# A two-layer decoder trunk on one core: stage changes rearranged, expert sums moved to TensorE, and unread matrix products placed in TensorE's gaps

## The chip, the cores and the metric

The kernel runs on one core of a Trainium2 chip. A core has five engines, each with its own instruction queue: TensorE (PE in the rows; its weight loads are PEld), VectorE (DVE), ScalarE (ACT), GpSimd (POOL) and SyncE (SP), which only starts transfers. They wait for one another by semaphores. The metric is the device time of one execution in microseconds, the median of three runs.

## The reference

The input is one sequence of 512 tokens of width 1024, in float32. There are two layers. Each is an attention part, a layer norm, a mixture of experts, and a second layer norm:

```
for i in range(DEPTH):
    mix = swa_sink_attention(...) if i % 2 == 0 else forgetting_attention(...)
    x = layer_norm(ALPHA * x + mix, ln_gain[i, 0], ln_bias[i, 0])
    ffn = grouped_moe(x, w_router, b_router, w_gate[i], w_up[i], w_down[i])
    x = layer_norm(ALPHA * x + ffn, ln_gain[i, 1], ln_bias[i, 1])
```

The router gives each token two of 16 experts and two gates. An expert computes `silu(x @ w_gate) * (x @ w_up)`, 256 wide, and multiplies that by `w_down`. The token's `ffn` is the sum of its two experts' rows, each times its gate.

## The kernel before

**Layout.** The 512 tokens are `NT = 4` tiles of 128 rows; `xres` holds them, 1024 columns each. Precise products of float32 data are made of three products of split operands (`three`, lines 491 to 493): high by high, high by low, low by high. `KC = 8` steps of three, 24 products of 512 columns, are one **group**. The splits are made by ScalarE (the high part, a cast) and VectorE (the low part, a subtraction).

**Order of a layer.** Input projection, attention, output projection (`wo_done`), first norm, routing, experts, second norm. After each tile's first norm TensorE transposes it (`turn_x`, line 477), and multiplies it by the router weights (`route`, line 648, products 16 columns wide). A long chain of small VectorE instructions then picks experts (`asn_b`, semaphore `assigned`), TensorE ranks the tokens by two products (674, 675), VectorE works out their places, TensorE turns these into row numbers (680), and GpSimd starts an indirect DMA for each expert (line 429) that fetches its 96 token rows from `xd` in HBM into `xe`. TensorE transposes the rows (`turn_rows`, 687), ScalarE and VectorE split them (`evac_rows`, lines 925 and 1336), and TensorE runs the gate and up products as one group of 24 (`gate_up_split`), the transposes of the hidden rows (706) and the down products (713, eight of 512 columns on plain float32).

**The expert loop.** A step `step(i, u)` has expert e's gate/up group, then the transposes for expert e+1 and the down products of expert e-1. The splits of expert e+1's weights are ScalarE's line 904 and VectorE's 1222, in four parts. The weights lie in a ring of four slots of 3 MB; SyncE's queue loads them ahead, in order, 1 MB each for gate, up and down. Between steps 2 and 3 ScalarE's queue has four instructions that multiply `xres` by ALPHA (line 959). Finished rows go to `ys` in HBM (line 920).

**After the experts.** GpSimd waits until all rows are stored, reads a counter (`n_ovf`), and gathers for each tile the two rows of each token (`gather`, line 458) into `gy`, with buffers for two tiles, so that the gathers of tiles 2 and 3 wait for `mixed`. VectorE adds the two, times their gates, to `xres` (lines 1415 and 1418), and norms (`norm`, 1027 to 1042); GpSimd computes the reciprocal root in two instructions (387, 388). In layer 0 the next layer's projection follows: `turn_x`, the split of the tile (`state_high`, `state_low`), and two groups of 24 products a tile. The projection's weights are split meanwhile (990 and `value_weights_low`, 1396). In layer 1 the four tiles are stored and the program ends. A branch for more than 96 tokens at one expert is in the program; the counter decides, and no row of the branch stands in the trace.

Of the kernel before, what the change touches and what calls it, by code (L numbers as in the profile page):

```python
# [48 lines left out]
def trunk(nc, x, ln_gain, ln_bias, swa_w_in, swa_sinks, swa_w_o, fox_w_in, fox_b_f, fox_w_o,  # L49
# [8 lines left out]
    with ctx:  # L58
# [95 lines left out]
        gy = area(0, 4 * D, "p (b k n) -> p b k n", b=2, k=2)  # L154
# [89 lines left out]

        block = ctx.enter_context(nc.Block())
# [3 lines left out]
        def _(eng):  # L249
# [33 lines left out]
            for l, (w_in, w_o) in enumerate(((swa_w_in[0], swa_w_o[0]), (fox_w_in[0], fox_w_o[0]))):  # L283
                for j in range(IN_BLOCKS[l]):
                    c = IN_ORDER[l][j]
                    if l == 1 and j == 2:

                        for b in range(2):
                            eng.wait_ge(S(f"gy_in0{b}"), 64)
# [53 lines left out]
        def _(eng):  # L343
# [39 lines left out]
            def norm_rstd(l, w, gather=None):  # L383
# [16 lines left out]
            for l in range(DEPTH):  # L400
# [30 lines left out]
                eng.wait_ge(S("placed"), l + 1)  # L431
                for b in range(2):
                    eng.wait_ge(S(f"y_stored{l}{b}"), 16 * NE // 2)
                n_ovf = eng.value_load(ovf_id[0:1, OVF:OVF + 1], min_val=0, max_val=OVF)
# [18 lines left out]
                def gather(t):  # L453

                    if t >= 2:
                        eng.wait_ge(S(f"mixed{l}"), t - 1)
                    for k in range(TOPK):
                        eng.indirect_dma_start(gy[:, t % 2, k, :], None, ys,
                                               bass.IndirectOffsetOnAxis(ap=pos[:, t, k:k + 1], axis=0)).then_inc(S(f"gy_in{l}{t % 2}"), 16)
                gather(0)  # L460
                gather(1)
                norm_rstd(l, 1, gather)


        @block.tensor
        def _(eng):
            def turn_x(t, a):
# [5 lines left out]
                if t >= 1:  # L473
                    eng.wait_ge(S(f"xt_act{a}"), t)
                    eng.wait_ge(S(f"xt_dve{a}"), t)
# [3 lines left out]
                mm.then_inc(S(f"xt_done{a}"), 1)  # L479

            eng.wait_ge(S("ident"), 1)
            turn_x(0, "in")
            for l in range(DEPTH):

                def xT_here(a, t):
                    eng.wait_ge(S(f"xt_act{a}"), t + 1)
                    eng.wait_ge(S(f"xt_dve{a}"), t + 1)

# [6 lines left out]
                if l == 0:  # L495
# [9 lines left out]
                    for j in range(IN_BLOCKS[0]):  # L505
                        for t in range(NT):
                            k = NT * j + t
                            xT_here("in", t)
                            if k >= 2:
                                eng.wait_ge(S(f"proj_free{l}{k % 2}"), k // 2)  # L510
                            for c in range(KC):
                                if k < NT - 1 and c == KC // 2:
# [9 lines left out]
                else:  # L522

                    turn_x(0, "01")
# [935 lines left out]
```

## Time and profile before

| | us |
|---|---|
| median of 3 runs | 988.99 (987.59 to 992.05) |
| the profiled execution | 988.5 |
| its span, first to last instruction | 986.6 |
| TensorE busy, of the span | 829.8 (84%) |
| VectorE / ScalarE / GpSimd busy | 547.7 / 383.9 / 136.1 |
| mean granted TensorE clock | 0.919 |

The granted clock is a share of 2.4 GHz; a stretch at 0.50 is one at 1.2 GHz. A window of the profile with, say, 0.54 has both levels in it. The mean of 0.919 says that TensorE had the lower level for about 16% of the span.

### The profile page before, as it was taken

Reading aid. Unit: us, or ns where it says so; the run is one execution under the profiler, and the core shown is the slowest. Engines: PE = TensorE matmul, PEld = TensorE weight load, DVE = VectorE, ACT = ScalarE, POOL = GpSimd, SP = SyncE. Lnnn points to the kernel's source line nnn. Section 1 sums busy time; section 2 is a strip of 40 time slices with the busy share of each in tenths; the row PEclk is TensorE's granted clock in tenths of the full one; section 3 lists DMA queues with packets and bytes.
Section 4 is the critical chain, followed back from the end, with each engine's and each line's share of the span. In section 5 each row is a group of like instructions: output and inputs, shape, how many; then the busy total and the mean of one; then the engine's idle time right before and its main releaser. Section 6 shows DMA issues by size and latency. Waiting matters only on the chain.

```text
span 986.6 us, 11641 instructions
## 1 busy us (share of the span) xinstructions
PE 829.8 (84%) x4140; PEld 601.7 (61%) x4140; DVE 547.7 (56%) x1086; ACT 383.9 (39%) x763; POOL 136.1 (14%) x153
## 2 busy tenths in 40 slices
PE   6999999981989999818999999999981889999910
PEld 4887777871546565417878877887861556556500
DVE  4534884556557676366332225664556556767437
ACT  4323884002455555231222226775001365555300
POOL 2000221121001000032000002221111100100033
PEclk9999999985899999959999999999985799999965
DMA  9942000149699998645062223111139599999144
GB/s 320 349 138 86 2 1 1 43 170 336 189 353 332 360 353 316 219 141 183 30 215 86 86 86 107 65 44 44 43 119 360 151 340 340 361 357 374 42 124 158
DMA packets 106851, 183.11 MB, mean 186 GB/s; under 512 B 6496, under 2 KB 72032, under 8 KB 106800
## 3 DMA queue, kind: packets, MB, share of 16 engines
q1 hardware_dynamic: 92864, 132.34, 39.7%
q0 software_dynamic: 9200, 33.33, 10.9%
q10 hardware_dynamic: 4736, 16.78, 4.5%
q8 instruction: 29, 0.48, 0.2%
q14 instruction: 22, 0.18, 0.1%
HBM read 159.60 MB, written 22.84 MB: 185 GB/s over the span
## 4 chain that ended last, share of the span: by engine, by line
PE 81%; DVE 9%; DMA 4%; issue 3%; POOL 2%; ACT 1%; POOLq 0%; DVEq 0%; SPq 0%; ACTq 0%
PE bank L491 16%; PE bank L492 16%; PE bank L493 16%; PE bank L713 12%; PE bank L613 5%; PE bank L579 4%; PE bank L596 3%; PE bank L687 2%; PE bank L477 2%; DMA arena<-xd,row_ids 1%; PE bank L648 1%; POOL veps L387 1%; DVE xres L1042 1%; DMA arena<-ys,pos 1%; PE bank L621 1%
## 5 line engine op out<-in xcount | busy, mean ns | idle before, releaser
L1222 DVE TENSOR_TENSOR low<-ring,gu_high 128x1024 fp32r<-128x1024 f32 x128 | 151.2, 1221 | 50.6 <-ACT gu_high L904 50.6
L904 ACT CAST gu_high<-ring 128x1024 fp32r<-128x1024 f32 x128 | 127.7, 1049 | 16.8 <-DVE arena L1353 16.8
L713 PE MATMUL bank<-ring,arena 128*96 128x512 f32 x256 | 119.8, 611 | 11.3 <-issue 9.2
L491 PE MATMUL bank<-gu_high,rows_high 128*96 128x512 f32 x256 | 115.4, 451 | 8.2 <-DVE rows_low L1336 8.2
L492 PE MATMUL bank<-low,rows_high 128*96 128x512 f32 x256 | 103.6, 405 | 0.0
L493 PE MATMUL bank<-gu_high,rows_low 128*96 128x512 f32 x256 | 103.0, 402 | 0.0
L713 PEld LDWEIGHTS bank<-ring,arena 128*96 128x96 f32 x256 | 40.1, 167 | 67.7 <-issue 67.3
L852 ACT ACTIVATE arena<-arena,nmax 128x256 f32<-128x256 f32 (+3 forms) x128 | 66.8, 522 | 30.8 <-DVE nmax L1153 20.0
L491 PE MATMUL bank<-high,x_high 128*128 128x512 f32 x160 | 66.2, 414 | 10.3 <-DVE low L1048 5.1
L414 POOL TENSOR_TENSOR low<-ring,high 128x512 fp32r<-128x512 f32 x32 | 40.6, 1269 | 231.1 <-ACT high L872 231.1
L613 PE MATMUL bank<-arena 128*128 128x64 f32 x544 | 68.1, 269 | 0.2 <-ACT arena L866 0.2
L613 PEld LDWEIGHTS bank<-arena 128*128 128x128 f32 x544 | 65.8, 192 | 0.5 <-ACT arena L866 0.5
L429 POOL DMA_INDIRECT arena<-xd,row_ids x32 | 30.2, 944 | 258.2 <-PE bank L687 220.0
L492 PE MATMUL bank<-low,x_high 128*128 128x512 f32 x160 | 64.7, 404 | 0.0
L493 PE MATMUL bank<-high,xlow 128*128 128x512 f32 x160 | 64.6, 404 | 0.0
L491 PEld LDWEIGHTS bank<-gu_high,rows_high 128*96 128x96 f32 x256 | 42.9, 167 | 33.3 <-DVE rows_low L1336 9.1
L492 PEld LDWEIGHTS bank<-low,rows_high 128*96 128x96 f32 x256 | 42.7, 167 | 23.7 <-issue 7.9
L493 PEld LDWEIGHTS bank<-gu_high,rows_low 128*96 128x96 f32 x256 | 42.7, 167 | 19.2 <-issue 0.9
L491 PE MATMUL bank<-high,attn_high 128*128 128x512 f32 x128 | 51.5, 402 | 0.0
L493 PE MATMUL bank<-high,attn_low 128*128 128x512 f32 x128 | 51.3, 401 | 0.0
L491 PE MATMUL bank<-x_high,wsplit 128*128 128x512 f32 x128 | 50.8, 397 | 0.0
L492 PE MATMUL bank<-xlow,wsplit 128*128 128x512 f32 x128 | 50.8, 397 | 0.0
(207 smaller groups left out, 1399.2 us busy)
## 6 DMA issues: line engine op xcount, KB each, us to landing
ring<-in_w_gate SPq DMA_DIRECT2D x32, 1024.0 KB, 12.3
ring<-in_w_up SPq DMA_DIRECT2D x32, 1024.0 KB, 14.4
ring<-in_w_down SPq DMA_DIRECT2D x32, 1024.0 KB, 12.7
ys<-arena ACTq DMA_DIRECT2D x32, 384.0 KB
ring<-in_fox_w_in SPq DMA_DIRECT2D x6, 2048.0 KB, 10.7
ring<-in_swa_w_in SPq DMA_DIRECT2D x3, 2048.0 KB, 8.8
ring<-in_swa_w_o SPq DMA_DIRECT2D x2, 2048.0 KB, 17.4
xd<-xres ACTq DMA_DIRECT2D x8, 512.0 KB, 2.6
```

Of the source, the lines that this page charges most:

```text
L414: eng.tensor_tensor(low, w, high, ALU.subtract).then_inc(S(f"out_low{l}"), 1)
L429: eng.indirect_dma_start(xe[0:CAP, e % RING, :], None, xd, bass.IndirectOffsetOnAxis(ap=row_ids[:, e:e + 1], axis=0)).then_inc(S(f"xe_in{l ...
L491: eng.matmul(out, ah, wh, start=(c == 0), stop=False)
L492: eng.matmul(out, ah, wl, start=False, stop=False)
L493: return eng.matmul(out, al, wh, start=False, stop=(c == KC - 1))
L579: mm = eng.matmul(s_bank(s, half)[:, 0:nk], QT[r, hp, n * P:(n + 1) * P], KT[r, kp, k0 * P:k1 * P], start=True, stop=(l == 0))
L596: mm = eng.transpose(bank[3 + half][:, i * P:(i + 1) * P], sp[:, 2 * (s % 2) + half, i * P:(i + 1) * P], ident[:, :])
L613: mm = eng.matmul(bank[5 + hp % 2][:, at:at + HD], pT[:, half, i * P:(i + 1) * P], (V0 if l == 0 else V)[:, k0 + i, v:v + HD], start=(i == ...
L713: mm = eng.matmul(bank[5 + half][0:CAP, :], hT[:, b, c, :], w[:, c, half * BLK:(half + 1) * BLK], start=(c == 0), stop=(c == FC - 1))
L852: eng.activation(p, p, ACT.Exp, bias=nmax[:, hp % 2, n, half:half + 1], scale=-1.0, accum_out=rsum[:, hp % 2, n, half:half + 1]).then_inc( ...
L904: eng.copy(gu_high[u % 2][:, part, :], slot_in(use)[:, part, :]).then_inc(S("gu_high"), 1)
L1222: eng.tensor_tensor(lows[use % RING][:, part, :], slot_in(use)[:, part, :], gu_high[u % 2][:, part, :], ALU.subtract).then_inc(S("gu_low"), 1)
```

## The change

All three stage changes (first norm to experts, experts to next layer, experts to output) are rewritten:

- **Sums on TensorE.** VectorE builds `gate_diag`, eight 128x128 diagonal matrices of the gates. TensorE multiplies them with the gathered rows (`mix_rows`, four plain float32 products of 512 columns a tile), and VectorE adds `ALPHA * xres` from PSUM in two halves, with the statistics of each half between. The multiplication by ALPHA on ScalarE (959) goes. `gy` has room for all four tiles, so that all eight gathers are issued in a row, and the counter is read before the wait for the stores.
- **Norm.** VectorE adds LN_EPS itself; GpSimd has one instruction a tile in place of two.
- **Later fourth slot.** SyncE's queue holds the load of the ring's last slot (gate, up and down of expert 3) until the rows of expert 1 have landed.
- **Transposes within products.** Expert 1's rows are transposed in the middle of expert 0's group; splits signal per half. In the next layer's projection the waits are per half and `turn_x` and `mix_rows` stand between groups.
- **Unread products.** `hum(n, b)` issues n products of the bf16 identity with itself repeated, 512 columns wide, into a PSUM bank nobody reads: 12, 4, 26, 8 and 26 around the routing of each layer, 40 after each layer's experts, and 10 more in layer 0.

The core of the diff:

```diff
-        gy = area(0, 4 * D, "p (b k n) -> p b k n", b=2, k=2)
+        gy = area(0, NT * TOPK * D, "p (t k n) -> p t k n", t=NT, k=TOPK)
+        gate_diag = area(10112, NT * TOPK * P, "p (t k n) -> p t k n", t=NT, k=TOPK)
...
                 for u in range(RING):
                     k = EXP_USE[l] + u
+                    if u == RING - 1:
+                        eng.wait_ge(S(f"xe_in{l}1"), 16)
...
                     eng.wait_ge(S(f"ln_stats{l}{w}"), t + 1)
-                    link(eng.tensor_scalar(veps[:, t:t + 1], mv[:, t, 1:2], LN_EPS, None, ALU.add))
                     eng.tensor_tensor(rstd[:, t:t + 1], veps[:, t:t + 1], mhalf[:, t:t + 1], ALU.pow).then_inc(S(f"rstd{l}{w}"), 1)
-                    if gather and t + 2 < NT:
-                        gather(t + 2)
...
+            def hum(n, b=5):
+                for i in range(n):
+                    eng.matmul(bank[b][:, :], ident_b[:, :], ident_b[:, :].unsqueeze(1).to_broadcast([P, NT, P]),
+                               start=True, stop=True)
...
+            def mix_rows(l, t):
+                eng.wait_ge(S("diag_ready"), l + 1)
+                eng.wait_ge(S(f"gy_in{t}"), 32 * (l + 1))
+                if t >= 2:
+                    eng.wait_ge(S(f"added{l}"), 2 * (t - 1))
+                for b in range(2):
+                    for k in range(TOPK):
+                        mm = eng.matmul(mix_bank(t, b)[:, :], gate_diag[:, t, k, :], gy[:, t, k, b * BLK:(b + 1) * BLK],
+                                        start=(k == 0), stop=(k == TOPK - 1))
+                    mm.then_inc(S("mixed"), 1)
...
+                    eng.wait_ge(S("y_act0"), NE)
+                    hum(40)
+                    mix_rows(0, 0)
+                    mix_rows(0, 1)
+                    hum(10, 0)
                     turn_x(0, "01")
...
                                 mm = three(bank[b][:, :], x1_high[:, c, cols], xlow[:, c, cols], wh, wl, c)
                             mm.then_inc(S(f"proj_done{l}"), 1)
-                        if t == 0:
-                            turn_x(1, "01")
+                            if b == 0 and t + 2 < NT:
+                                mix_rows(0, t + 2)
...
                     for c in range(KC):
+                        if c % (KC // 2) == 0:
+                            eng.wait_ge(S(f"xeT_dve{l}"), 2 * e + (1 + c // (KC // 2)))
+                        if first and c == KC // 2:
+                            eng.wait_ge(S(f"xe_in{l}1"), 16)
+                            turn_rows(1).then_inc(S(f"xeT_done{l}"), 1)
...
-                eng.wait_ge(S("x_stored"), 16 * NT * (l + 1))
-                for t in range(NT):
-                    eng.activation(xres[:, t, :], xres[:, t, :], ACT.Copy, scale=ALPHA).then_inc(S(f"scaled{l}"), 1)
...
+                for t in range(NT):
+                    for k in range(TOPK):
+                        ins = eng.tensor_scalar(gate_diag[:, t, k, :], ident[:, :], gates[:, t, k:k + 1], None, ALU.mult)
+                ins.then_inc(S("diag_ready"), 1)
...
                 if l + 1 < DEPTH:
-                    value_weights_low(0, KC)
+                    value_weights_low(0, 2 * KC)
                 for t in range(NT):
...
+                    for b in range(2):
+                        eng.wait_ge(S("mixed"), 2 * (NT * l + t) + b + 1)
+                        v = xres[:, t, b * BLK:(b + 1) * BLK]
+                        eng.scalar_tensor_tensor(v, v, ALPHA, mix_bank(t, b)[:, :], ALU.mult, ALU.add).then_inc(S(f"added{l}"), 1)
```

Three places show what the queues hold. TensorE's queue at the routing of layer 0, before (`xres` transposes, router products on `wr`, ranks on `asn_b`, row numbers on `id_part`, then the first expert's rows):

```order
L648 MATMUL bank<-wr,xT 128x16 x7
L477 MATMUL bank<-ident,xres 128x128 [waits xt_dve00,xt_act00,x_ready00]
L477 MATMUL bank<-ident,xres 128x128 x7
L648 MATMUL bank<-wr,xT 128x16 [waits xt_dve00,xt_act00]
L648 MATMUL bank<-wr,xT 128x16 x7
L674 MATMUL bank<-asn_b,before_b 128x64 [waits assigned]
L675 MATMUL bank<-asn_b,ones_b 128x64
L680 MATMUL bank<-id_part,place_is 96x16 [waits places_ready]
L680 MATMUL bank<-id_part,place_is 96x16 x7
L687 MATMUL bank<-ident,arena 128x96 [waits xe_in00]
```

and the same place after the change (the unread products are line 469):

```order
L469 MATMUL bank<-ident_b 128x512 x12
L483 MATMUL bank<-ident,xres 128x128 [waits xt_dve00,xt_act00,x_ready00]
L678 MATMUL bank<-wr,xT 128x16 [waits xt_dve00,xt_act00]
L678 MATMUL bank<-wr,xT 128x16 x7
L469 MATMUL bank<-ident_b 128x512 x4
L469 MATMUL bank<-ident_b 128x512 [waits shifted]
L469 MATMUL bank<-ident_b 128x512 x25
L708 MATMUL bank<-asn_b,before_b 128x64 [waits assigned]
L469 MATMUL bank<-ident_b 128x512 x8
L715 MATMUL bank<-id_part,place_is 96x16 [waits places_ready]
L469 MATMUL bank<-ident_b 128x512 x26
L722 MATMUL bank<-ident,arena 128x96 [waits xe_in00]
```

Every wait of TensorE here now has unread products ahead of it. TensorE's queue between layer 0's experts and the projection of layer 1 had only the branch for many tokens and then the transposes:

```order
L713 MATMUL bank<-ring,arena 96x512 x3
L759 REGISTER_ALU
L759 COMPARE_AND_BRANCH
L756 UNCONDITIONAL_BRANCH
L477 MATMUL bank<-ident,xres 128x128 [waits x_ready01]
L477 MATMUL bank<-ident,xres 128x128 x7
L491 MATMUL bank<-high_61,x_high 128x512 [waits v_low,xt_dve01,xt_act01]
```

and now has (line 495 is `mix_rows`):

```order
L469 MATMUL bank<-ident_b 128x512 [waits y_act0]
L469 MATMUL bank<-ident_b 128x512 x39
L495 MATMUL bank<-arena 128x512 [waits gy_in0,diag_ready]
L495 MATMUL bank<-arena 128x512 x3
L495 MATMUL bank<-arena 128x512 [waits gy_in1,diag_ready]
L495 MATMUL bank<-arena 128x512 x3
L469 MATMUL bank<-ident_b 128x512 x10
L483 MATMUL bank<-ident,xres 128x128 [waits x_ready01]
```

The transposes of tile 0 stand behind the sums of tiles 0 and 1 and 50 unread products. VectorE's last tile of the program, before:

```order
L1415 SCALAR_TENSOR_TENSOR xres<-arena,gates,xres 128x1024 [waits gy_in11]
L1418 SCALAR_TENSOR_TENSOR xres<-arena,gates,xres 128x1024 [waits dve_step]
L1027 BN_STATS stats<-xres 128x6 [waits mixed1]
L1027 BN_STATS stats<-xres 128x6
L1038 BN_AGGR mv<-stats 128x2 [waits dve_step]
L1040 SCALAR_TENSOR_TENSOR xres<-xres,mv,lnp 128x1024 [waits ln_stats11]
L1042 SCALAR_TENSOR_TENSOR xres<-xres,rstd,lnp 128x1024 [waits rstd11,dve_step]
```

and after:

```order
L1458 SCALAR_TENSOR_TENSOR xres<-xres,bank 128x512 [waits mixed]
L1070 BN_STATS stats<-xres 128x6 [waits added1]
L1458 SCALAR_TENSOR_TENSOR xres<-xres,bank 128x512 [waits mixed,dve_step]
L1070 BN_STATS stats<-xres 128x6 [waits added1]
L1078 BN_AGGR mv<-stats 128x2 [waits dve_step]
L1079 TENSOR_SCALAR veps<-mv 128x1 [waits dve_step]
L1080 SCALAR_TENSOR_TENSOR xres<-xres,mv,lnp 128x1024
L1082 SCALAR_TENSOR_TENSOR xres<-xres,rstd,lnp 128x1024 [waits rstd11,dve_step]
```

Two sums of 1024 columns became two of 512 that read PSUM, and one small addition is new.

## Rows read from the trace of the kernel before

**Rows 1.** Windows: stretch, its length, engines' busy time, granted clock, DMA share, GB/s.

```profile
225.00:250.00 25.00, 7.42 (x30) 5.31 (x31) 16.70 (x64) 3.12 (x5) 4.68 (x5) 0.50 0.89 283
...
325.00:350.00 25.00, 24.83 (x112) 15.44 (x111) 18.00 (x23) 14.69 (x21) 1.94 (x3) 1.00 1.07 356
...
425.00:450.00 25.00, 9.96 (x31) 7.94 (x32) 17.89 (x24) 4.28 (x9) 8.03 (x8) 0.54 0.39 125
```

**Rows 2.** Timeline, TensorE, layer 0's stage change: start, duration, instruction, [idle before <-releaser].

```profile
215.68 1.97 PE L477 MATMUL bank<-ident,xres 128*128 128x128 f32 x8 [3.59 <-DVE xres L1042]
218.52 3.57 PE L648 MATMUL bank<-wr,xT 128*128 128x16 f32 x16 [0.88 <-DVE xT L1012]
229.75 0.24 PE L674 MATMUL bank<-asn_b,before_b 128*128 128x64 bf16 x1 [7.66 <-DVE asn_b L1283]
233.40 0.81 PE L680 MATMUL bank<-id_part,place_is 128*96 128x16 f16 x8 [3.36 <-DVE place_is L1300]
241.60 1.54 PE L687 MATMUL bank<-ident,arena 96*128 96x96 f32 x8 [7.39 <-DMA arena<-xd,row_ids]
245.22 0.74 PE L491 MATMUL bank<-gu_high,rows_high 128*96 128x512 f32 x1 [2.08 <-DVE rows_low L1336]
252.94 0.82 PE L687 MATMUL bank<-ident,arena 96*128 96x96 f32 x8
255.77 0.48 PE L491 MATMUL bank<-gu_high,rows_high 128*96 128x512 f32 x1 [2.01 <-DVE rows_low L1336]
```

**Rows 3.** Timeline, VectorE's norm and GpSimd's first gather, same stretch.

```profile
214.34 1.28 DVE L1042 SCALAR_TENSOR_TENSOR xres<-xres,rstd,lnp 128x1024 f32<-128x1024 f32 x1 [0.84 <-POOL rstd L388]
...
235.31 1.01 POOL L429 DMA_INDIRECT arena<-xd,row_ids  x1 [18.20 <-DVE row_ids L1303]
```

**Rows 4.** Timeline, TensorE, first expert's transposes in layer 1.

```profile
764.47 1.54 PE L687 MATMUL bank<-ident,arena 96*128 96x96 f32 x8 [9.15 <-DMA arena<-xd,row_ids]
```

**Rows 5.** Timeline, TensorE and ScalarE, expert steps 1 to 4 of layer 0.

```profile
262.97 0.33 PE L706 MATMUL bank<-ident,arena 96*128 96x96 f32 x2
...
278.73 3.90 ACT L959 ACTIVATE xres<-xres 128x1024 f32<-128x1024 f32 x4 [0.51 <-DVE arena L1353]
...
282.99 0.33 PE L706 MATMUL bank<-ident,arena 96*128 96x96 f32 x2
...
287.46 5.29 PE L713 MATMUL bank<-ring,arena 128*96 128x512 f32 x8 [3.48 <-issue]
...
298.12 0.33 PE L706 MATMUL bank<-ident,arena 96*128 96x96 f32 x2
```

**Rows 6.** Timeline, all engines, from layer 0's experts into layer 1.

```profile
413.89 3.65 PE L713 MATMUL bank<-ring,arena 128*96 128x512 f32 x8 [0.92 <-DVE arena L1343]
...
420.24 4.91 DVE L1396 TENSOR_TENSOR low<-ring,high 128x512 fp32r<-128x512 f32 x8 [1.99 <-ACT high L990]
...
424.49 1.48 POOL L458 DMA_INDIRECT arena<-ys,pos  x1 [0.30 <-issue]
...
429.76 1.28 DVE L1415 SCALAR_TENSOR_TENSOR xres<-arena,gates,xres 128x1024 f32<-128x1024 f32 x1 [4.61 <-DMA arena<-ys,pos]
...
442.01 0.77 PE L491 MATMUL bank<-high,x_high 128*128 128x512 f32 x1 [2.53 <-issue]
...
495.35 0.40 PE L491 MATMUL bank<-x_high,wf_parts 128*16 128x512 f32 x1
```

**Rows 7.** Line 458, its first gather, at 423.1: issue to landing.

```profile
DMA to landing us min/median/max: 4.3/4.3/4.3
```

**Rows 8.** Groups: busy, mean ns of one, idle before: a sum from PSUM.

```profile
L1229 DVE SCALAR_TENSOR_TENSOR xres<-xres,bank 128x512 f32<-128x512 f32 x16 | 11.0, 688 | 48.8 <-PE bank L493 48.8
```

**Rows 9.** Timeline, VectorE, the last stage of the program.

```profile
951.98 1.28 DVE L1415 SCALAR_TENSOR_TENSOR xres<-arena,gates,xres 128x1024 f32<-128x1024 f32 x1 [11.28 <-DMA arena<-ys,pos]
...
959.58 1.27 DVE L1415 SCALAR_TENSOR_TENSOR xres<-arena,gates,xres 128x1024 f32<-128x1024 f32 x1
...
981.00 1.28 DVE L1042 SCALAR_TENSOR_TENSOR xres<-xres,rstd,lnp 128x1024 f32<-128x1024 f32 x1 [0.83 <-POOL rstd L388]
```

More of the change, by code:

```diff
@@ L452, in _ @@
                         eng.wait_ge(S(f"ov_stored{l}"), 16 * j + 16)
[L453 to L456 removed]
+                for t in range(NT):
                     for k in range(TOPK):
[L458 to L462, printed above, removed]
+                        eng.indirect_dma_start(gy[:, t, k, :], None, ys,
+                                               bass.IndirectOffsetOnAxis(ap=pos[:, t, k:k + 1], axis=0)).then_inc(S(f"gy_in{t}"), 16)
+                norm_rstd(l, 1)
         @block.tensor
         def _(eng):
+            def hum(n, b=5):
+                for i in range(n):
+                    eng.matmul(bank[b][:, :], ident_b[:, :], ident_b[:, :].unsqueeze(1).to_broadcast([P, NT, P]),
+                               start=True, stop=True)
             def turn_x(t, a):
@@ L473, in turn_x @@
                 if t >= 1:
-                    eng.wait_ge(S(f"xt_act{a}"), t)
-                    eng.wait_ge(S(f"xt_dve{a}"), t)
+                    parts = 1 if a in ("00", "10") else 2
+                    eng.wait_ge(S(f"xt_act{a}"), parts * t)
+                    eng.wait_ge(S(f"xt_dve{a}"), parts * t)
                 for c in range(KC):
@@ L529, in _ @@
                             k = 2 * t + b
-                            if b == 1 and 1 <= t < NT - 1:
+                            if b == 1 and t < NT - 1:
                                 turn_x(t + 1, "01")
@@ L720, in step @@
                     e = 4 * i + u
-                    eng.wait_ge(S(f"xeT_dve{l}"), e + 1)
-                    gate_up_split(e, u % 2, use).then_inc(S(f"gu_done{l}"), 1)
+                    gate_up_split(e, u % 2, use, first).then_inc(S(f"gu_done{l}"), 1)
                     if not first:
@@ L725, in step @@
                         turn_h((u - 1) % 2).then_inc(S(f"hT_done{l}"), 1)
-                    if not last:
+                    if not first and not last:
                         eng.wait_ge(S(f"xe_in{l}{(u + 1) % 4}"), 16 * i + 16 * ((u + 1) // 4) + 16)
@@ L768, in _ @@
                         down(0, EXP_USE[l] + NE).then_inc(S(f"ov_turn{l}"), 1)
+            eng.wait_ge(S("y_act1"), NE)
+            hum(40)
+            for t in range(NT):
+                mix_rows(DEPTH - 1, t)
         @block.scalar
@@ L942, in step @@
                         gate_up_high(i, u + 1, 0, 3)
+                    if first:
+                        evac_rows(1, 1)
                     silu(e, u % 2)
                     if not last:
-                        evac_rows(e + 1, (u + 1) % 2)
+                        if not first:
+                            evac_rows(e + 1, (u + 1) % 2)
                         gate_up_high(i, u + 1, 3, SPLITS)
@@ L997, in _ @@
                             eng.copy(V[:, t, b * BLK:(b + 1) * BLK], bank[b][:, :]).then_inc(S(f"proj_free1{b}"), 1)
-                            if b == (1 if t == 0 else 0) and t + 1 < NT:
+                            if b == 0 and t + 1 < NT:
                                 state_high(t + 1)
@@ L1360, in step @@
                         evac_hT(e - 1, (u - 1) % 2)
+                    else:
+                        evac_rows(1, 1)
                     times_up(e, u % 2)
+                    if not first and not last:
+                        evac_rows(e + 1, (u + 1) % 2)
                     if not last:
-                        evac_rows(e + 1, (u + 1) % 2)
                         gate_up_low(i, u + 1, 3, SPLITS)
```

90 lines of the change are left out of this document (43 added, 47 removed).

## The prediction

> **What bounds the kernel now.** I read the windows first, then the timeline of the stretches that stand out. In most of the span TensorE is the bound: 24.83 us of 25 busy at 325 to 350, at the full clock [rows 1]. The stage changes are different. At 225 to 250 TensorE is busy for 7.4 of 25 us and has 1.2 GHz, at 425 to 450 for 10.0 with a clock of 0.54 [rows 1]. There the path is a chain: norm, transposes, router products, VectorE's choice, row numbers, gather, transposes, split [rows 2, 3]. It costs twice: TensorE waits, and what it does next runs at the lower clock. Eight row transposes take 1.54 us there, and 0.82 us one group later [rows 2]. The last stage is VectorE's alone, four tiles of 7.60 us [rows 9]. So time can come from shorter chains and from the clock. I place all times in the frame of the old trace.
>
> **Prices.** A product of 512 columns in a group: expert steps repeat every 10.01 us [rows 5], a step being 24 such products, eight down products and ten short transposes. The down products take 3.65 us, 0.43 each behind the first [rows 6]; the transposes about 1.0 (0.82 and two more, [rows 2, 5]). That leaves about 5.6 us, 0.23 each. An unread bf16 product has no row. Bounds: not less than the two 64-column bf16 products' share of a column, taken as 0.20; not more than the 0.23 of the split product if the clock is full, and twice that, 0.46, at 1.2 GHz. I take 0.22 at full clock, since it has the same columns as the split product.
>
> **First norm to second expert, layer 0.** Adding LN_EPS on VectorE removes the 0.84 us wait for GpSimd [rows 3] and adds about 0.25: x ready 0.6 earlier. TensorE idled 3.59 us before 215.68 [rows 2]; now 12 unread products (2.6 us) cover most of that, so that it should still have 2.4 GHz. Then the eight transposes take about 1.0 and not 1.97, the router products about 1.8 and not 3.57: 0.6 + 0.95 + 1.7 = 3.25 us. VectorE's choice (7.66 us of TensorE idle, [rows 2]) is unchanged; 30 unread products need 6.6 at full clock, and fit. If the clock fell during the short products, the first eight or so cost double and they end at about 8.2, 0.5 late. I book that 0.5. The next 8 (1.8) fit in 3.36. Then 26 (5.7 us) stand before the row transposes, where the wait was 7.39 us.
>
> The gather took 6.3 us, from 235.31 to 241.60 [rows 2, 3], while the fourth slot's 3 MB were still arriving. Held back, it should look like the gather of rows 7, 4.3 us: 2.0 saved. The 26 products end just after the landing, 0.3 later. Then, from 241.60 to the end of the second group at 262.97, 21.4 us [rows 2, 5]. After: 0.8 transposes, 1.25 for one half's split (half of the 2.08 wait plus a signal), 5.6 products with 0.8 transposes inside, 5.6 products: 14.1. The second 2.01 us wait goes because VectorE and ScalarE split expert 1's rows under four remaining steps of the first group (2.8 us for about 2.0 of work). Saved 7.3. Sum: 3.25 - 0.5 + 0.3 (row numbers at full clock) + 2.0 - 0.3 + 7.3 = **12.1**.
>
> **The same in layer 1.** The wait for the gather was 9.15, not 7.39 [rows 4, 2], with the same transfers in its way: 1.8 more, **13.9**.
>
> **ALPHA on ScalarE.** The four scalings (3.90 us) stand before the casts of the next weights. The step from 282.99 to 298.12 takes 15.13 us against 10.01; the down products waited 3.48 and ran at a lower clock, 5.29 for 3.65 [rows 5]. Gone: 5.1 a layer, **10.2**. What is late next is nobody: the other steps have no such wait.
>
> **Experts to layer 1.** The counter read before the stores saves about 0.6 us of the gather's start. The eight diagonals cost VectorE 1 to 2.4 us (0.13 to 0.3 each); I take 1.6. It now makes all 16 low parts ahead of the sums; eight took 4.91 [rows 6], so it is free at about 430.9, while the first sums (gather at 429.2, two products of 0.43) are ready at 430.1. Per tile VectorE then needs 5.95 us (below) and x is ready at 436.9. TensorE: 40 unread products from about 418.3, when the last down products (ended by 417.5, [rows 6]) have been copied out, end at 427; sums of tiles 0 and 1, 1.7 each; 10 unread, 2.2, end at 436.6, just under. Transposes 1.0, one half split 1.4: the first group starts at 439.4, not 442.01 [rows 6]. From there to 495.35 were 53.3 us. After: eight groups 44.6, three transposes 2.8, sums of tiles 2 and 3 now in TensorE's path 3.4, together 50.8. Saved 2.6 + 2.5 = **5.1**.
>
> **The last stage.** A tile took 7.60 us [rows 9]. Out: two sums of 1024 columns (1.3 each) and the 0.83 wait for GpSimd; in: two sums from PSUM of 0.69 [rows 8] with links, 1.5, and 0.25 for LN_EPS. 7.60 - 3.45 + 1.8 = 5.95. Four tiles save 6.6. Against that the first sum waits for two products, 0.9 to 1.7; the earlier counter gives 0.6. GpSimd issues its eight gathers about 1.4 us apart (423.1 and 424.49, [rows 7, 6]), and so is done about when tile 0 needs its root. Net **6.0**.
>
> **Sum.** 12.1 + 13.9 + 10.2 + 5.1 + 6.0 = 47.3 us. The edits in the first projection (waits by half) I cost at nothing: its products wait there on weights. The profiled execution took 988.5 (span 986.6 and 1.9 around it), 0.5 under the median: 941.2. The full clock is assumed everywhere, and in each of the three changes there is some stretch of short products or waiting in which it can fall. I allow 2 us for all of these together: **943**.
>
> **A rule that speaks against it.** The transposes at 241.60 and the products at 218.52 ran at 1.2 GHz throughout, with TensorE working in most of 215.7 to 222.1, and the clock rose only after wide products, within the group that began at 245.22 [rows 2]. The Trainium skill (page "TensorE: Matmul & The Clock Gate", Part 4: PE-mode transpose) says that the full clock does not engage for transposes. By the first half of that the 26 unread products before 241.60 would do nothing for the transposes themselves; but 0.82 against 1.54 [rows 2] shows transposes at either level, so the trace decides, and only the question whether short work holds the clock stays open.
>
> **Rivals.**
> 1. *Weights become the bound.* A step moves 3.1 MB of weights, 0.4 MB of gathered rows and 0.4 MB of stores: 391 GB/s for a 10.0 us step, while the DMA gives 356 at a share of 1.07 [rows 1]. The backlog grows by a microsecond a step. With the fourth slot late, all of slot 3 to expert 15's up weights, 48 MB, must come from about 238 on: 136 us at 356 GB/s, landing at 374. Expert 15's weights are first wanted at about 262.97 - 12.1 + 12 steps + 5.7 = 376.7. It fits by 2 to 3 us. At 340 GB/s it lands at 379.5 and costs up to 3; if row gathers also suffer, 4 to 8 a layer: 951 to 959. Chance 0.13.
> 2. *Unread products end late.* By my times at 0.22 each they end within half a microsecond of what they cover. With one cold stretch in each of five places, 1.5 to 3 us each: 951 to 958. Chance 0.10.
> 3. *Slower.* If unread products neither hold nor raise the clock, each costs 0.46. The 12 end 2.5 us late, the 30 another 6.2, the 26 end at 254.8 where the rows now start at 241.60. Each layer's change loses 9.8; the 40 end at 436.7, and with 10 more the layer change loses about 9; the last stage loses 2. Against the 10.2 of ALPHA: 20 us slower, 1009. It decides from about 0.39 us a product on. Against it: wide products do raise the clock now, 24 of them from 245.22 to 252.94 in 7.7 us and not 11 [rows 2]. Chance 0.03.
> 4. *GpSimd is held up.* With VectorE at its low parts one gather issue took 1.48 us, not the 1.01 of the first row gather [rows 6, 3]. Now they run beside all eight, which costs about 0.5 a gather; it hides behind VectorE's own 430.9. The Trainium skill (page "SBUF — State Buffer", section "SBUF: two separate sides") says that VectorE can hold the port that GpSimd needs to write descriptors. If that were full, the gathers would land 5.3 us after 430.9 and the layer change would give nothing: 948. Rows speak against it. Chance 0.04.
>
> **Range and chances.** The forecast, 934 to 951, has 0.66; below 934 (first group sooner, no cold stretch) 0.04. Range of 8 in 10: 933 to 959. A measurement of this kernel tells about 0.5% (5 us) from no change. Only rival 3 is slower, and rivals 1 and 2 together would still be 20 us faster. Faster 0.95, same 0.02, slower 0.03.
>
> **What would show it.** Right: granted clock 1.00 in most windows of the stage changes; first expert's gather near 4.5 us; no 15 us step; first group of layer 1 about 2.6 us (beyond the earlier gains) sooner; tiles of the last stage 5.95 us apart. Wrong: ScalarE's casts of weights waiting for DMA late in the experts; `assigned` or the row landing earlier than the last unread product by over a microsecond; sums waiting for products. The prediction falls if the unread products run at 0.46, or if the weight stream sets the pace.

## The result, and the profile after

The changed kernel takes 963.5 us (median of 4 runs, 962.4 to 965.0) where the one before took 990.5 in the same session (4 runs, 987.6 to 993.3): a ratio of 0.973, 95% interval 0.971 to 0.975. The forecast was 943 with a range to 959, so the sign was right and a large part of the gain was missing. The profiled execution took 965.0 us, its span is 963.2 against 986.6: 23.4 us saved there, half of the 47.3 in my sum.

The windows of [rows 1], now (columns as there):

```profile
225.00:250.00 25.00, 22.12 (x117) 13.05 (x116) 18.15 (x57) 6.90 (x10) 5.53 (x6) 1.00 0.79 234
325.00:350.00 25.00, 24.44 (x101) 14.66 (x100) 15.90 (x20) 12.01 (x17) 1.81 (x2) 1.00 1.07 350
425.00:450.00 25.00, 23.51 (x100) 16.39 (x99) 16.43 (x25) 3.32 (x6) 4.58 (x3) 1.00 0.48 175
```

The clock is full in all three; it was 0.50 and 0.54 in the first and the last. In the first the unread products are the cause: without them (no_hum, below) the same window has 0.57. The last shows less than it seems to, since the same work now stands 11.65 us earlier in the frame. The window of like work is 413.35 to 438.35; it has 0.93 here and 0.78 in no_hum, so the new order of the work did one part of it and the unread products another. The timeline of TensorE through layer 0's stage change, beside [rows 2]:

```profile
210.92 2.75 PE L469 MATMUL bank<-ident_b 128*128 128x512 bf16 x12
214.39 1.09 PE L483 MATMUL bank<-ident,xres 128*128 128x128 f32 x8 [0.72 <-DVE xres L1082]
216.36 2.81 PE L678 MATMUL bank<-wr,xT 128*128 128x16 f32 x16 [0.88 <-DVE xT L1055]
219.01 9.10 PE L469 MATMUL bank<-ident_b 128*128 128x512 bf16 x30
...
231.19 0.53 PE L715 MATMUL bank<-id_part,place_is 128*96 128x16 f16 x8 [1.30 <-DVE place_is L1339]
231.57 5.77 PE L469 MATMUL bank<-ident_b 128*128 128x512 bf16 x26
237.18 0.84 PE L722 MATMUL bank<-ident,arena 96*128 96x96 f32 x8
242.47 0.82 PE L722 MATMUL bank<-ident,arena 96*128 96x96 f32 x8
251.46 0.33 PE L746 MATMUL bank<-ident,arena 96*128 96x96 f32 x2
```

The second expert's group ends at 251.46, 11.5 us sooner. 26 unread products take 5.77 us, 0.22 each, and transposes take 0.82 and 1.09 where they took 1.54 and 1.97. The 30 took 9.10 instead of 6.6: the clock was at 1.2 GHz for part of them. SyncE's queue now holds the fourth slot back: from 230 to 234 the DMA moved 3 GB/s on average, where it moved 350 in the trace before.

Now the place where the gain went. The timeline of ScalarE, VectorE and TensorE around the thirteenth expert of layer 0:

```profile
351.13 2.94 ACT L949 CAST gu_high<-ring 128x1024 fp32r<-128x1024 f32 x3 [3.33 <-DMA ring<-in_w_up]
352.21 3.50 DVE L1261 TENSOR_TENSOR low<-ring,gu_high 128x1024 fp32r<-128x1024 f32 x3 [4.31 <-ACT gu_high L949]
352.58 0.33 PE L746 MATMUL bank<-ident,arena 96*128 96x96 f32 x2
...
356.08 5.34 PE L753 MATMUL bank<-ring,arena 128*96 128x512 f32 x8 [2.51 <-issue]
```

The cast of the weights waits 3.33 us for their DMA, the low part waits for the cast, and the down products are late and fall to 1.2 GHz, 5.34 us for 3.65. The next row of line 746 is at 366.79, 14.2 us after 352.58 instead of 10.0. Layer 1 has the same (14.35). The page's part on DMA issues (KB each, us to landing) has the weights' own part of it:

```profile
ring<-in_w_up SPq DMA_DIRECT2D x32, 1024.0 KB, 16.4
```

In the median they land 16.4 us after their issue. A wait like this is found by listing the distances between equal instructions of a loop, one of which stands out; in the page it is only the DMA item of the chain.

The sums after the experts of layer 0 on TensorE and VectorE, and the second and third tile's:

```profile
406.55 8.81 PE L469 MATMUL bank<-ident_b 128*128 128x512 bf16 x40 [0.67 <-ACT arena L981]
418.19 8.80 PE L495 MATMUL bank<-arena 128*128 128x512 f32 x16 [2.83 <-DMA arena<-ys,pos]
...
437.15 3.59 PE L495 MATMUL bank<-arena 128*128 128x512 f32 x8
```

```profile
421.60 0.69 DVE L1458 SCALAR_TENSOR_TENSOR xres<-xres,bank 128x512 f32<-128x512 f32 x1 [3.12 <-issue]
...
423.67 0.69 DVE L1458 SCALAR_TENSOR_TENSOR xres<-xres,bank 128x512 f32<-128x512 f32 x1 [0.65 <-PE bank L495]
...
427.25 1.28 DVE L1082 SCALAR_TENSOR_TENSOR xres<-xres,rstd,lnp 128x1024 f32<-128x1024 f32 x1 [0.55 <-POOL rstd L393]
```

A tile has four products in the code and x8 in the trace, 3.59 us. One plain float32 product of 512 columns is two records of 0.43 us, 0.86 in all.

Measured where I had booked it, from rows of the same kind in both traces (before: the last pair of line 706 in each layer at 412.63 and 935.08, layer 1's second group at 785.56; after: line 746 at 400.98, 913.25 and 763.81):

| stretch | booked | saved |
|---|---|---|
| up to the router products of the third tile, layer 0 | 0 | 1.0 |
| from there to the second expert, layer 0 | 12.1 | 10.5 |
| its other experts (ALPHA) | 5.1 | 0.1 |
| experts to the end of layer 1's eight groups (485.65) | 5.1 | -2.0 |
| attention and output projection of layer 1 | 0 | -1.5 |
| norm to the second expert, layer 1 | 13.9 | 13.6 |
| its other experts (ALPHA) | 5.1 | 0.1 |
| last stage | 6.0 | 1.6 |

The first line's 1.0 is no gain. That row is at 209.22 here and at 210.23 before; light_stream has it at 210.54 with the code of the changed kernel, and before_no_alpha at 209.15 with the old one.

### The profile page after: what moved, and what is told of

Its sections match the earlier page's. It is cut to its first block, busy times and chain, and to the rows that moved or that the text cites. A ratio compares the mean times of both kernels' runs of the same rounds, so it can differ in the third digit from the quotient of the medians.

```text
span 963.2 us, 12330 instructions
## 1 busy us (share of the span) xinstructions
PE 900.6 (93%) x4446; PEld 626.3 (65%) x4446; DVE 544.8 (57%) x1118; ACT 376.6 (39%) x755; POOL 125.6 (13%) x137
## 4 chain that ended last, share of the span: by engine, by line
PE 81%; DMA 6%; DVE 6%; issue 3%; POOL 1%; SPq 1%; ACT 1%; POOLq 0%; DVEq 0%; ACTq 0%
PE bank L514 15%; PE bank L515 15%; PE bank L516 15%; PE bank L753 11%; PE bank L643 5%; PE bank L609 4%; DMA ring<-in_w_up 4%; PE bank L626 3%; PE bank L469 2%; PE bank L495 2%; PE bank L722 2%; PE bank L483 1%; PE bank L678 1%; DMA arena<-ys,pos 1%; PE bank L651 1%
## 5 line engine op out<-in xcount | busy, mean ns | idle before, releaser
L753 PE MATMUL bank<-ring,arena 128*96 128x512 f32 x256 | 120.0, 613 | 10.4 <-issue 6.9
L514 PE MATMUL bank<-gu_high,rows_high 128*96 128x512 f32 x256 | 112.4, 439 | 3.2 <-DVE rows_low L1375 3.2
L515 PE MATMUL bank<-low,rows_high 128*96 128x512 f32 x256 | 101.2, 395 | 0.0
L516 PE MATMUL bank<-gu_high,rows_low 128*96 128x512 f32 x256 | 100.4, 392 | 0.0
L469 PE MATMUL bank<-ident_b 128*128 128x512 bf16 x242 | 58.0, 400 | 1.3 <-ACT arena L981 1.3
L515 PE MATMUL bank<-low,attn_high 128*128 128x512 f32 x128 | 50.9, 398 | 0.0
## 6 DMA issues: line engine op xcount, KB each, us to landing
ring<-in_w_up SPq DMA_DIRECT2D x32, 1024.0 KB, 16.4
ring<-in_fox_w_in SPq DMA_DIRECT2D x6, 2048.0 KB, 11.2
```

Of the source, the lines that this page charges most:

```text
L469: eng.matmul(bank[b][:, :], ident_b[:, :], ident_b[:, :].unsqueeze(1).to_broadcast([P, NT, P]), start=True, stop=True)
L514: eng.matmul(out, ah, wh, start=(c == 0), stop=False)
L515: eng.matmul(out, ah, wl, start=False, stop=False)
L516: return eng.matmul(out, al, wh, start=False, stop=(c == KC - 1))
L753: mm = eng.matmul(bank[5 + half][0:CAP, :], hT[:, b, c, :], w[:, c, half * BLK:(half + 1) * BLK], start=(c == 0), stop=(c == FC - 1))
```

## The experiments

All are compared with the kernel before on the same chip, in four sessions, so kernels are compared with each other by their ratios. The last two columns are read from the timelines: the time from the second expert's group to the last expert (the rows of the table above), where a stream that never holds anything up gives 144.7.

| kernel | us | ratio (95%) | experts, layer 0 | layer 1 |
|---|---|---|---|---|
| before | 990.5 | 1 | 149.7 | 149.5 |
| changed | 963.5 | 0.973 (0.971 to 0.975) | 149.5 | 149.4 |
| early_slot | 963.9 | 0.971 (0.970 to 0.973) | 144.9 | 144.8 |
| alpha_back | 963.1 | 0.972 (0.970 to 0.973) | 150.8 | 151.0 |
| light_stream | 952.9 | 0.961 (0.959 to 0.963) | 144.8 | 144.7 |
| hum50 | 959.0 | 0.967 (0.966 to 0.969) | 148.8 | 149.9 |
| no_hum | 965.5 | 0.975 (0.972 to 0.977) | 145.8 | 150.3 |
| one_product | 954.0 | 0.963 (0.961 to 0.965) | 147.4 | 147.0 |
| split_slot | 955.4 | 0.964 (0.962 to 0.965) | 146.1 | 144.8 |
| combo2 | 950.3 | 0.959 (0.957 to 0.961) | 145.1 | 149.5 |
| before_no_alpha | 980.8 | 0.990 (0.989 to 0.992) | 144.7 | 144.5 |
| light_no_hum | 964.2 | 0.974 (0.972 to 0.976) | 145.0 | 144.8 |
| combo3 | 961.0 | 0.971 (0.969 to 0.973) | 144.8 | 144.8 |

**alpha_back.**

```diff
+                eng.wait_ge(S("x_stored"), 16 * NT * (l + 1))
+                for t in range(NT):
+                    eng.activation(xres[:, t, :], xres[:, t, :], ACT.Copy, scale=ALPHA)
```

(VectorE's sums then multiply by 1.0 in place of ALPHA.)

> The changed kernel with the four scalings by ALPHA back on ScalarE where they stood before, between the third and the fourth expert (the later sums then multiply by 1). Theory W: ScalarE's pause gives the weight stream 5 us to catch up, so a step of 15.1 us appears at the fourth expert, and the 14.2 us step at the fourteenth is gone or much shorter: 964 to 966. Rival A (the 10.2 us that I booked for ALPHA came in, and were lost elsewhere): 973 to 974, with both long steps in each layer.

The time is the same. Its timeline of TensorE has the long step back. Counted as above it is the step of the fifth expert; the expectation's "fourth" and "fourteenth" are the fifth and the thirteenth here:

```profile
270.78 0.33 PE L746 MATMUL bank<-ident,arena 96*128 96x96 f32 x2
...
275.20 6.27 PE L753 MATMUL bank<-ring,arena 128*96 128x512 f32 x8 [3.44 <-issue]
...
286.84 0.33 PE L746 MATMUL bank<-ident,arena 96*128 96x96 f32 x2
```

That is 16.1 us, and no later step is over 10.4. The median of 963.1 is 1 us below what theory W gave, and 10 below rival A. One pause takes the place of the other: theory W.

**light_stream.**

```diff
-                eng.dma_start(slot_down(s), w_down[w, e].rearrange("(c p) n -> p c n", p=P)).then_inc(sem, 16)
+                n = D // 2 if isinstance(e, int) and e >= RING else D
+                eng.dma_start(slot_down(s)[:, :, 0:n], w_down[w, e][:, 0:n].rearrange("(c p) n -> p c n", p=P)).then_inc(sem, 16)
```

> The changed kernel, but from the fifth expert on only half of the columns of the down weights are loaded (0.5 of 3 MB an expert left out; these products read older weights). Theory W: the stream never falls behind, no step above 10.1 us after the first expert: 8.4 to 8.8 us less in all, 955. Rival E (the 14.2 us step comes from the engines' own order and not from DMA): 963.5, step unchanged.

No step exceeds 10.4 us and each layer's experts take 4.7 us less; the whole is some 12 us faster by the ratios, 10.6 by the medians. 9.4 of these are the stream; for the rest, the sums found the full clock at both places here, which the changed kernel's profile didn't (hum50, below).

**before_no_alpha.**

```diff
-                eng.wait_ge(S("x_stored"), 16 * NT * (l + 1))
-                for t in range(NT):
-                    eng.activation(xres[:, t, :], xres[:, t, :], ACT.Copy, scale=ALPHA).then_inc(S(f"scaled{l}"), 1)
```

(VectorE's wait for `scaled` goes too.)

> The kernel before with one edit: ScalarE's four scalings by ALPHA left out in each layer (the scaling is missing from the result). Theory S (stream and late slot together eat the gain): when the second expert's group ends, the old kernel's stream is 2.2 MB (6.3 us) further ahead than the changed kernel's, more than the 5.1 us of the scalings. So here both steps of 15 us fall to 10.1 and no other step grows: 10.2 us saved, ratio 0.9897. Rival T (the stream always takes this gain, whatever stands before it): a step at the twelfth to fifteenth expert grows by 4 us a layer, 1 to 3 us saved, ratio 0.997 to 0.999.

It came out as theory S says: 9.5 us saved (ratio 0.990), with both steps of 15 us gone and none grown; each layer's experts take 5.0 us less. So the price of 5.1 us a layer was right, and in the old kernel it could be had.

**early_slot.**

```diff
-                    if u == RING - 1:
-                        eng.wait_ge(S(f"xe_in{l}1"), 16)
```

> The changed kernel, but the fourth slot's weights (3 MB) are again loaded without waiting for expert 1's row gather. Theory W (the weight stream became the bound): the 3 MB no longer stand in the stream that runs at 350 GB/s from 240 us on, a backlog smaller by some 8 us, which is more than the 4.2 us by which the one step of 14.2 us in each layer exceeds the others. That step is gone: 8.4 to 8.6 us saved; the row gather of expert 0 is in the transfers again, 2.0 us in layer 0 and 3.8 in layer 1, so that about 3 us are left: 960 to 961 against 963.5. Rival G (my prediction's own account, in which the late slot is worth 3.8 us and the stream has room): 967, and the 14.2 us step stays.

The long step is gone, as W says, but the time did not move: 963.9 lies between the two forecasts. The row gather paid more than the 2.0 us that both theories gave it:

```profile
232.04 0.99 POOL L430 DMA_INDIRECT arena<-xd,row_ids  x1 [15.76 <-DVE row_ids L1340]
...
240.84 0.88 PE L720 MATMUL bank<-ident,arena 96*128 96x96 f32 x8 [2.58 <-DMA arena<-xd,row_ids]
```

8.8 us from issue to use, at most 4.4 in the changed kernel, where the 26 unread products hide all of it. In the trace before, the gather was issued at 235.31 and landed at 241.60; here it is issued 3.3 us sooner and lands 0.8 us sooner. The slot's weights still move while it runs (the weights' queue has 0.32 MB from 238 to 240 here and 0.24 before, 0.10 and nothing from 240 to 242), so a gather that is issued sooner waits longer. The second expert's group ends at 257.59 instead of 251.46: waiting with the slot is worth 6.1 us in layer 0 (and 5.6 in layer 1) and costs 4.6 of stream a layer.

**split_slot.**

```diff
                     if u == RING - 1:
-                        eng.wait_ge(S(f"xe_in{l}1"), 16)
-                    if u >= OUT_BLOCKS:
+                        eng.dma_start(slot_in(k)[:, :, 0:F], w_gate[l, u]...).then_inc(S(f"w_loaded{k % RING}"), 16)
+                        eng.wait_ge(S(f"xe_in{l}0"), 16)
+                        eng.dma_start(slot_in(k)[:, :, F:2 * F], w_up[l, u]...).then_inc(S(f"w_loaded{k % RING}"), 16)
+                    elif u >= OUT_BLOCKS:
```

> The changed kernel, but of the fourth slot's weights the gate part (1 MB) is loaded without a wait and the other 2 MB after the first row gather instead of the second: the stream is 2.9 + 1.8 = 4.7 us further at the same moment. Theory W: that is more than the 4.2 us for which the fourteenth expert's step waits, so that no step exceeds 10.6 us; the gather of expert 0 overlaps 1 MB at its start and lands 0 to 1 us later: 955 to 957 against 963.5. Rival G (any transfer beside the row gather costs it what the whole slot cost, 4 us and more): 963 to 965, with the long step gone.

955.4, as theory W had it (I miscounted the expert in the expectation: it is the thirteenth). One step of 11.2 us is left in layer 0, and none in layer 1. The gather still lands in time, at 4.7 us:

```profile
231.97 0.99 POOL L434 DMA_INDIRECT arena<-xd,row_ids  x1 [15.66 <-DVE row_ids L1344]
...
236.66 0.37 SPq L319 DMA_DIRECT2D ring<-in_w_up  x1
236.68 0.88 PE L724 MATMUL bank<-ident,arena 96*128 96x96 f32 x8 [0.17 <-issue]
```

**combo3.** The same split, but gate and up parts both ahead of the wait, with combo2's other edits.

> combo2, but of the fourth slot the gate and up parts (2 MB) are loaded without a wait and only the down part after the first row gather: the stream is 2.9 us further again, so the step of 14.1 us that combo2 still showed in layer 1 (4.2 us) shrinks to 11 or less. Against it: 2 MB in the way of the first row gather instead of 1 (which cost it 0.3 us). Theory W: 947 to 949 against 950.3. Rival G (2 MB cost the gather 2 us a layer and more, as the whole slot cost it 4.4): 950 to 952.

Rival G was right, by more than it said: some 11 us slower than combo2 by medians and by ratios, though its experts are as short as they can be (144.8 and 144.8). The gather of layer 0 took 7.1 us (233.06 to 240.14), that of layer 1 8.1 (742.99 to 751.13), and layer 1's transposes then ran at 1.2 GHz:

```profile
751.13 1.54 PE L722 MATMUL bank<-ident,arena 96*128 96x96 f32 x8 [3.55 <-DMA arena<-xd,row_ids]
```

One MB ahead of the gather costs it 0.3 us in layer 0, two cost 2.7, three 4.4; in layer 1 it took 4.4 at most with none ahead, 4.8 with one, and 8.1 with two as with three. What goes with it is how long the weights still arrive behind the gather's issue: in layer 0 of split_slot (issue at 231.97) the DMA's rate has fallen to 153 GB/s in 232 to 234, in combo3 (issue at 233.06) it is at 334 up to 236. That this is the cause is my reading; no run here moves the gather alone.

**no_hum.**

```diff
-                for i in range(n):
+                for i in range(0):
                     eng.matmul(bank[b][:, :], ident_b[:, :], ...
```

> The changed kernel without any of the unread products (126 a pass over the two layers and the end, none left). Theory C (they are worth what the clock gives back): transposes, router products and row numbers of the first norm's tail at 1.2 GHz again (3 us a layer), row transposes and the first part of the first expert's group (2.5 a layer), sums, transposes and first group after the experts (3.5), first sums of the last stage (nothing, they ran at 1.2 GHz anyway): 978, and the granted clock below 0.95. Rival N (waits set the stage changes, the clock does not matter there): 963.5, within 2.

Left out are all 242 unread products, not 126 as the expectation counts. It is only 2 us slower, and the intervals allow from none to 5: rival N's time, and far from theory C's 978 (its profiled execution, 970.9, is 5 us above its median, so its absolute times are read with care). The clock is low again in the first norm's change, and the second expert's group of layer 0 ends 4.6 us later (256.05); but the last expert only 0.9 later (401.88 against 400.98), because the wait for weights shrank by 3.7. In layer 1 it did not.

**light_no_hum.** The edits of light_stream and no_hum together.

> light_stream without the unread products (half of the down weights' columns are left out from the fifth expert on, so that the stream cannot hold anything up). Theory S: leaving out the unread products cost only 2 us in the changed kernel because the later start was given back by a shorter wait for weights. Without that wait their full worth shows: 4.6 a layer in the first norm's tail and first experts, about 1.4 after the experts of layer 0, 0.5 at the end: 11 us more than light_stream's 953, 964. Rival N (they are worth 2 us anywhere): 955.

964.2, a ratio of 0.974 against light_stream's 0.961: 13 us by the ratios, 11.4 by the medians. Theory S holds. The 242 unread products are worth 11 to 13 us where the stream has room, and about 2 where it has none.

**hum50.**

```diff
-                    hum(40)
+                    hum(50)
```

(and the same at the end)

> The changed kernel with 50 unread products instead of 40 ahead of the expert sums, in both layers. Theory C: the sums' first products ran at 1.2 GHz because TensorE idled 2.8 and 2.3 us before them; 50 products end at 417.5 and 929.8, about where the gather lands, the clock stays, and the sums of tile 0 are ready 1.2 to 1.8 us earlier at both places: 960.0 to 961.0. Rival D (the gather or VectorE ends the wait, or the clock falls there anyway): 963.5, within 0.5.

959.0, some 5.7 us less by the ratios; both intervals together allow 3 to 9. In the last stage the sums start at once at the full clock:

```profile
927.43 10.54 PE L495 MATMUL bank<-arena 128*128 128x512 f32 x24
```

In the changed kernel it was

```profile
929.94 12.23 PE L495 MATMUL bank<-arena 128*128 128x512 f32 x24 [2.31 <-DMA arena<-ys,pos]
```

and the first addition came 3.2 us after the products' start (929.94 to 933.11), not 2.0 (927.43 to 929.42). Other traces qualify theory C. In the six profiles with 40 unread products (changed, early_slot, alpha_back, light_stream, split_slot, one_product) TensorE idled 1.7 to 3.0 us ahead of the sums at two places each. The clock had fallen at four of the twelve: both places of the changed kernel, the first of early_slot (2.90 us) and the second of one_product (3.04). It had held behind gaps of up to 2.68. In the three with 50 and at most 0.7 us of idle it fell at none of six. A short gap may cost the clock; it need not.

Where the clock held, ten more products gained nothing. From the last expert of layer 0 to the end of layer 1's eight groups alpha_back, light_stream and split_slot take 82.6 to 83.0 us and hum50 82.7, the changed kernel 84.7; behind the last expert of the program they take 47.6 to 48.0 us and hum50 48.2, the changed kernel 50.0. So one fall costs about 2 us at either place.

**one_product.**

```diff
-                    for k in range(TOPK):
+                    for k in range(1):
```

(Each product then starts and ends its own sum.)

> The changed kernel, but each tile's expert sum has only the product of the first expert (the second expert's share is left out), so that a tile has two products of 512 columns instead of four. Theory F (a plain float32 product of 512 columns takes 0.86 to 0.9 us, twice what I had read): four tiles give 1.8 each where TensorE is on the path (tiles 2 and 3 of layer 0 within the first groups of layer 1), tile 0 at both places 1.8 to 2.5: 7 to 8 us less, 956. Rival P (the price of 0.43 was right and the sums wait for something else): half of that, 960.

954.0, 9.5 us less (0.963 against 0.973). The two sums inside layer 1's first groups take 1.88 us, not 3.59; layer 1's first group starts 27.05 us after the last expert, not 30.54. Together 6.9, of which some 2 because these sums found the full clock. Theory F holds, since the two inside the groups are exactly halved. The wait for weights was shorter too, by 4.5 us in the two layers of this profile, which I didn't expect: it differs from profile to profile. (The profiled execution, 951.3, is the fastest of five.)

**combo2.** split_slot, hum50, and in the last stage

```diff
+                if w == 1 and l + 1 == DEPTH and t + 1 < NT:
+                    eng.wait_ge(S("mixed"), 2 * (NT * l + t + 1) + 1)
+                    n = xres[:, t + 1, 0:BLK]
+                    eng.scalar_tensor_tensor(n, n, ALPHA, mix_bank(t + 1, 0)[:, :], ALU.mult, ALU.add).then_inc(S(f"added{l}"), 1)
                 eng.wait_ge(S(f"rstd{l}{w}"), t + 1)
```

with that addition left out of its old place.

> split_slot and the 50 unread products together, and in the last stage VectorE adds the first half of the next tile between the two steps of the norm, where it waited 0.53 us for GpSimd's root (three times). By the measured parts: 963.5 - 7.5 (stream, if theory W holds) - 4 to 5 (50 products) - 1.6 = 950. If rival G holds for the gather: 957.

950.3 us, the fastest version, 4.1% below the kernel before. In the last stage's timeline of VectorE the root is waited for only in the last tile, and tiles are 5.6 us apart instead of 6.2:

```profile
929.95 0.69 DVE L1086 SCALAR_TENSOR_TENSOR xres<-xres,bank 128x512 f32<-128x512 f32 x1
930.55 1.28 DVE L1088 SCALAR_TENSOR_TENSOR xres<-xres,rstd,lnp 128x1024 f32<-128x1024 f32 x1
```

Its profile still has a step of 14.1 us in layer 1 where split_slot's has none, so the stream has just enough room and not always that.

## Why the prediction was wrong, step by step

**ALPHA on ScalarE** (booked 10.2, came 0.2) is the step that failed. The price was right (before_no_alpha), the sentence "What is late next is nobody" was not: the weights were. This is my rival 1, which I gave 0.13. Its inputs were right: the demand of a step, the 3 MB of the late slot, 350 GB/s (356 booked). Two things in its arithmetic were not. I tested only the last expert, and the wait came at the thirteenth. And its bound was too kind by rounding: the weight blocks in the page are of 1024 KB, so that the "48 MB" are 50 of the MB in which GB/s are counted, 141 us at 356 GB/s and not 136; even by my own times they landed at 379 and the last expert was late by 2 us, not early by as much. Neither the late slot nor the missing scalings did it alone. early_slot and before_no_alpha lack the scalings and do not hold the slot back, and both run their experts in 144.5 to 144.9. alpha_back holds the slot back and has the scalings, and it has no wait later than theirs.

**First norm to second expert** (26.0 booked for both layers, 24.1 came) was right, and for the right reasons in most parts. The late slot was undersized (6.1 us in layer 0, not 2.0; 5.6 in layer 1, not 3.8), since a gather that is issued sooner lands hardly sooner while the slot's weights arrive (early_slot). The price of a product came out at 0.23 although its sum does not: 10.01 less 3.65 and 1.0 leaves 5.4 us, not 5.6. Against this, the full clock didn't last: the router products took 2.81 us, the 30 products 9.10 and ended 1.2 us after the choice was ready. The wait of VectorE for GpSimd did not vanish, as booked, but went from 0.84 to 0.53, since the root now takes 1.52 us by itself:

```profile
L393 POOL TENSOR_TENSOR rstd<-veps,mhalf x16: 1515/1520/1549, 171.9 to 956.0; 128x1 f32<-128x1 f32 x16
```

**Experts to layer 1** (5.1 booked, -2.0 came): a mis-sized term. I read the x8 of the down products [rows 6] as eight products of 0.43, and called them eight in the description of the kernel; they are four in the code, two records each. The queue before shows it: `route` has 8 products a tile there (line 648) and x16 in [rows 2]. A tile's sums take 3.6 us and not 1.7: 3.8 of the 7.1 us are the two tiles in TensorE's path, and about 0.9 more the first tile's. The fallen clock at the sums took some 2 more, the wait for the root 0.5. one_product shows the first; the kernels whose clock held there show the second, and also that without the fall this change would have given nothing (82.6 to 83.0 us against 82.7 before). VectorE's 430.9 was added up 0.8 short besides: 420.24, twice 4.91 and 1.6 are 431.7. The Trainium skill (page "FP8 and Floating Point Precision", TensorE Precision Notes) says that true FP32 makes four passes; the runs agree, 0.86 us against the 0.22 of an unread bf16 product, and by that rule I would have had the right price.

**The last stage** (6.0 booked, 1.6 came) had the same two faults on its first tile. VectorE's first sum came 19.9 us after the last expert (933.11) and not 16.9 as before (951.98): 3.0 us lost, where I had 0.3 to 1.1. From there on 4.5 us were saved and not 6.6: the first tile took 7.1 us, as its second half waited 0.89 for TensorE, and the others 6.2, not 5.95, each with a wait of 0.5 for the root.

**Layer 1's attention** (0 booked, -1.5 came): the code is unchanged, and its first output products ran at 1.2 GHz, 670.97 to 674.4, after an idle of 0.84 us that the trace before has too, without the drop. Of the thirteen profiles, all with that code and that gap, it fell there in six (changed, early_slot, alpha_back, light_stream, hum50, combo2), for 1.3 to 1.6 us each. All six have unread products, as have three where it held (split_slot, one_product, combo3); in the four without any it never fell. Whether the unread products have a part in it or it is chance, these runs do not show. My 2 us for cold stretches were in the right place and too few: 1.0 and 1.2 in layer 0's change, about 2 at each of the two sums and 1.5 here make over 7.

**Rivals.** Rival 2 (unread products end late) cost 1.2 us at one place; the opposite, that they ended 2 to 3 us early, cost more. Rival 3 was excluded by 0.22 us a product at the full clock. Rival 4: beside VectorE's low parts the eight gathers stood 1.42, 1.78 and then 1.25 us apart, much as the first four did before, and held nobody up. Against the rule that the full clock does not engage for transposes (the Trainium skill, page "TensorE: Matmul & The Clock Gate", Part 4), transposes again ran at either level, 0.82 and 1.54 us for the same eight.

## What to carry to other kernels

Two edits that are each sound alone can fail together when they draw on the same slack. Where one delays a transfer and the other shortens the work that hides it, add up the stream expert by expert, not for the last one alone, and in the units of the profile. Count what one product in the code is in the trace before pricing it by a record. And if the clock is to be held over a gap, let the filling end at the landing and not 2 us before.

## What the runs showed of the hardware

- A plain float32 product of 512 columns took 0.86 us at the full clock, shown as two records of 0.43; the same shape in bf16 took 0.22.
- One core's DMA gave 344 to 348 GB/s at a share of 1.06 to 1.07 over the 110 us from 240 in five kernels (changed, light_stream, hum50, split_slot, combo2), and 347 to 356 over the 110 us from 760. The 356 GB/s of [rows 1] is the top of these.
- A GpSimd root of 128x1 took 0.57 us right behind an addition of 1.32, and 1.52 alone behind a wait: moving the addition away saved 0.4, not 1.3.
- The granted clock fell in 4 of 12 gaps of 1.7 to 3.0 us in like places, for about 2 us each time. Behind one gap of 0.84 us, the same in every kernel, it fell in 6 of 9 profiles with unread products and in none of 4 without, for 1.3 to 1.6 us each time.
- A row gather (0.4 MB) took 4.3 us from issue to use with no weights ahead of it (no_hum), and 7.1 to 8.8 with 2 or 3 MB of them still arriving.
